# Standing operands of the output and down projections at other byte offsets

## What is computed

```python
gates = jax.nn.sigmoid((h @ w_gate[l]).reshape(B, S, N_BRANCHES, D) + b_gate[l])
mixed = jnp.sum(gates * up, axis=2) @ w_out[l]          # w_out 2048 x 2048
x = x + rmsnorm(mixed, g[1])
h = rmsnorm(x, g[2])
m = jnp.square(jax.nn.relu(h @ w_up[l])) @ w_down[l]    # w_down 8192 x 2048
x = x + rmsnorm(m, g[3])
```

## The kernel before

| operand | role | offset |
|---|---|---|
| `op0h`, `op0l` (x0, x1, x2) | move in mode W, stand in mode T | 64 |
| `op1h`, `op1l` (pool, conv, mix, hidden, att, four) | move in mode W, stand in mode T | 64 |
| `whi`, `wlo` in mode T | move | 64 |
| `whi` in mode W | stands | 128 |
| `wlo` in mode W | stands | 0 |
| the region `big` (`mgh`, `hch`, `vx`, `qt` and others) | both | 64 |

## Time and profile before

### The profile page before, as it was taken

The page is one execution under the profiler, slowest core; times in us unless marked ns, Lnnn a source line. Parts: engine busy times, 40 slices in busy tenths (PEclk is TensorE's granted clock), DMA queues, the critical chain, the costliest instruction groups (busy, mean ns, idle before and its releaser), DMA issues.

```text
span 2187.2 us, 37567 instructions
## 1 busy us (share of the span) xinstructions
PE 2177.7 (100%) x15900; PEld 2046.9 (94%) x15900; DVE 1548.0 (71%) x1895; ACT 1063.0 (49%) x1398; POOL 120.0 (5%) x111
## 2 busy tenths in 40 slices
PE   9999999999999999999999999999999999999998
PEld 9999999999999889989988988998889999999987
DVE  7899588888889577544554555555768787777776
ACT  5444445544444566444543443444555555444443
POOL 1000000000000400000000000000101111110001
PEclk9999999999999999999999999999999999999999
DMA  8876676687787956656656656656755545688784
GB/s 275 245 241 200 201 251 220 228 280 258 256 277 265 244 188 184 193 192 194 196 195 193 194 193 196 200 192 203 246 174 164 164 144 170 224 272 282 256 279 155
DMA packets 248480, 474.97 MB, mean 217 GB/s; under 512 B 21974, under 2 KB 26448, under 8 KB 247544
## 3 DMA queue, kind: packets, MB, share of 16 engines
q1 hardware_dynamic: 243032, 454.40, 65.5%
q0 software_dynamic: 5280, 18.17, 2.9%
HBM read 468.30 MB, written 5.78 MB: 217 GB/s over the span
## 4 chain that ended last, share of the span: by engine, by line
PE 97%; DMA 1%; DVE 1%; ACT 0%; issue 0%; SPq 0%; DVEq 0%; POOLq 0%; POOL 0%; ACTq 0%
PE ps L917 21%; PE ps L918 21%; PE ps L919 21%; PE ps L910 10%; PE ps L911 10%; PE ps L912 10%; PE ps L835 1%; DMA raw<-in_w_out 1%; PE ps L758 0%; PE ps L708 0%; DMA raw<-in_w_in 0%; PE ps L745 0%; PE ps L824 0%; PE ps L823 0%; PE ps L825 0%
## 5 line engine op out<-in xcount | busy, mean ns | idle before, releaser
L917 PE MATMUL ps<-op0h,whiW 128*128 128x256 f32 x3376 | 937.3, 278 | 0.1
L919 PE MATMUL ps<-op0h,wloW 128*128 128x256 f32 x3376 | 932.8, 276 | 0.0
L918 PE MATMUL ps<-op0l,whiW 128*128 128x256 f32 x3376 | 932.7, 276 | 0.0
L1318 DVE TENSOR_TENSOR wloW<-raw,whiW 128x1024 fp32r<-128x1024 f32 (+1 forms) x503 | 618.3, 1241 | 313.5 <-ACT whiW L964 311.1
L964 ACT ACTIVATE whiW<-raw 128x1024 fp32r<-128x1024 f32 (+1 forms) x504 | 529.3, 1058 | 586.0 <-PE ps L919 471.2
L917 PEld LDWEIGHTS ps<-op0h,whiW 128*128 128x128 f32 x3376 | 633.8, 188 | 2.5 <-issue 1.3
L918 PEld LDWEIGHTS ps<-op0l,whiW 128*128 128x128 f32 x3376 | 633.9, 188 | 0.6
L919 PEld LDWEIGHTS ps<-op0h,wloW 128*128 128x128 f32 x3376 | 633.8, 188 | 0.0
L1318 DVE TENSOR_TENSOR wloT<-raw,whiT 128x1024 fp32r<-128x1024 f32 (+1 forms) x264 | 319.1, 1217 | 237.7 <-ACT whiT L964 236.5
L964 ACT ACTIVATE whiT<-raw 128x1024 fp32r<-128x1024 f32 (+1 forms) x264 | 274.0, 1046 | 286.2 <-PE ps L912 228.9
L910 PE MATMUL ps<-whiT,op1h 128*128 128x512 f32 x640 | 249.3, 390 | 0.3 <-DVE wloT L1318 0.3
(11 more groups left out here) (314 smaller groups left out, 2106.8 us busy)
## 6 DMA issues: line engine op xcount, KB each, us to landing
raw<-in_w_in SPq DMA_DIRECT2D x256, 512.0 KB, 4.3
raw<-in_w_up SPq DMA_DIRECT2D x128, 512.0 KB, 3.8
raw<-in_w_down SPq DMA_DIRECT2D x128, 512.0 KB, 4.1
raw<-in_w_ada SPq DMA_DIRECT2D x96, 512.0 KB, 4.6
raw<-in_w_gate SPq DMA_DIRECT2D x96, 512.0 KB, 5.1
raw<-in_w_out SPq DMA_DIRECT2D x64, 512.0 KB, 5.3
raw<-in_w_branch SPq DMA_DIRECT2D x48, 512.0 KB, 5.1
raw<-in_w_proj_a SPq DMA_DIRECT2D x24, 512.0 KB, 5.0
```

Of the source, the lines that this page charges most:

```text
L917: pe.matmul(o, wh, xh[:, ka, :], start=first and m % 2 == 0, stop=False, skip_group_check=True)
L918: pe.matmul(o, wh, xl[:, ka, :], start=False, stop=False, skip_group_check=True)
L919: mm = pe.matmul(o, wl, xh[:, ka, :], start=False, stop=last, skip_group_check=True)
L1318: v.tensor_tensor(wlo[job.mode][q % NSPL][:, :, 0:job.n], x, h.bitcast(F32), ALU.subtract).then_inc(s_lo, 1)
```

## The change

The activations' high and low parts of `mix` and of the four hidden blocks get tensors of their own that overlap `op1h` and `op1l` at shifted addresses. The offsets past a multiple of 256 (256 is the same as 0) are: `mix` 128 and 0 (high and low), `hid0` 128 and 0, `hid1` 0 and 128, `hid2` 64 and 192, `hid3` 192 and 64. 448 bytes are added behind. All instructions, waits and loads stay as they are.

```diff
         op1h, op1l = sb("op1h", [128, 16, 256], F32R), sb("op1l", [128, 16, 256], F32R)
+        def standing(name, high, low):
+
+            return (at(f"{name}h", [128, 16, 256], op1_at - 64 + high, F32R), at(f"{name}l", [128, 16, 256], op1_at + 16576 + low, F32R))
+
+        mixh, mixl = standing("mix", 128, 256)
+        hidden = [standing("hid_a", 128, 256), standing("hid_b", 256, 128), standing("hid_c", 64, 192), standing("hid_d", 192, 64)]
+        top[0] += 448
         tmp_at = top[0]
...
-        hi_of = {..., "mix": op1h, "hid0": op1h, "hid1": op1h, "hid2": op1h,
-                 "hid3": op1h, ...}
+        hi_of = {..., "mix": mixh, "hid0": hidden[0][0], "hid1": hidden[1][0], "hid2": hidden[2][0],
+                 "hid3": hidden[3][0], ...}
...
-                    act.activation(op1h[:, k:k + 2, :], mx[:, k:k + 2, :], ACT.Copy).then_inc(s_mixh, 1)
+                    act.activation(mixh[:, k:k + 2, :], mx[:, k:k + 2, :], ACT.Copy).then_inc(s_mixh, 1)
...
-                    act.activation(op1h[:, k:k + 2, :], half(tmp[2 + u % 4]), ACT.Copy).then_inc(s_hhi, 1)
+                    act.activation(hidden[blk][0][:, k:k + 2, :], half(tmp[2 + u % 4]), ACT.Copy).then_inc(s_hhi, 1)
```

More of the change, by code:

```diff
@@ L403, in program @@
         fgb = at("fgb", [128, 2048], op1_at)
[L404 to L407, removed]
+        hi_of = {"x0": op0h, "x1": op0h, "x2": op0h, "pool": op1h, "conv": op1h, "mix": mixh, "hid0": hidden[0][0], "hid1": hidden[1][0], "hid2": hidden[2][0],
+                 "hid3": hidden[3][0], "att": op1h, "four": op1h, "ya": yah, "ctx": hch, "mg": mgh}
+        lo_of = {"x0": op0l, "x1": op0l, "x2": op0l, "pool": op1l, "conv": op1l, "mix": mixl, "hid0": hidden[0][1], "hid1": hidden[1][1], "hid2": hidden[2][1],
+                 "hid3": hidden[3][1], "att": op1l, "four": op1l, "ya": yal, "ctx": hcl, "mg": mgl}
         columns = {}
@@ L1732, in ep_br @@
                         v.wait_ge(s_mixh, 2 * c + i + 1)
-                        v.tensor_tensor(op1l[:, k:k + 2, :], mx[:, k:k + 2, :], op1h[:, k:k + 2, :].bitcast(F32), ALU.subtract).then_inc(s_mix, 1)
+                        v.tensor_tensor(mixl[:, k:k + 2, :], mx[:, k:k + 2, :], mixh[:, k:k + 2, :].bitcast(F32), ALU.subtract).then_inc(s_mix, 1)
             def ep_wo(job, b0, b1):
@@ L1757, in ep_up @@
                     v.wait_ge(s_hhi, u + 1)
-                    v.tensor_tensor(op1l[:, k:k + 2, :], half(tmp[2 + u % 4]), op1h[:, k:k + 2, :].bitcast(F32), ALU.subtract).then_inc(s_hid, 1)
+                    h, l = hidden[blk]
+                    v.tensor_tensor(l[:, k:k + 2, :], half(tmp[2 + u % 4]), h[:, k:k + 2, :].bitcast(F32), ALU.subtract).then_inc(s_hid, 1)
             def ep_dn(job, b0, b1):
```

## The result

The changed kernel takes 2199.69 us (2199.32 to 2200.58) where the kernel before takes 2188.46 beside it: ratio 1.0051, 95% interval 1.0034 to 1.0069. It is 11 us slower; 9.7 us faster had been forecast. The span of the profiled execution is 2198.1 us.

What follows compares the result with a forecast made beforehand. TensorE's matmul spacing was taken as the bound; 7.68 + 2.56 - 0.56 = 9.7 us gained, giving 2179.3 us against the profiled execution and a median of 2178.9 us (-0.44%), range 2175.0 to 2189.4.

Steps and rivals of the forecast that it cites:

- What bounds the kernel: Whole kernel: matmul spacing on TensorE sets the time, busy 2177.7 of 2187.2 us; neither loads nor VectorE or ScalarE do.
- That the address sets the pitch, by the distance to the moving operand: TensorE matmuls: each standing-tile load takes 16 cycles from the moving stream, 16 more if at the moving operand's offset.
- The strided tile of `ub`: 512-column matmuls at 64 and 64, standing tile spread over twice the bytes: 233.3 ns, 48 cycles over, so loads aren't hidden.
- Distance 64 at -6.67 ns: Output and down projections: 1152 matmuls moved to distance 64 save 6.67 ns each, 7.68 us.
- A distance of 64 either way: `mix`, `hid0`, `hid1`: standing at 128 or 0 counts alike, both 64 from the moving operand.
- 384 matmuls unchanged: `hid2` and `hid3`: 256 and 128 matmuls stay at 64 and were counted as unchanged.
- Distance 128 as for 64: `hid2` and `hid3`: 384 matmuls moved to 192 taken at -6.67 ns each, 2.56 us gained.
- the third rival: 512-column matmuls: whole excess goes for every tile leaving 64, 1536 x 13.3 ns; 2169.1 us, chance 0.05.
- The gap in `wo0`: Output projection: some 84 faster matmuls only reach a late chunk earlier; gap grows some 0.5 us, 0.56 us gain lost.
- Writes and what lies behind at nothing: VectorE and ScalarE writes (at most 4 us uncovered) and moved temporaries (-0.2 to +1.3 us) both costed at zero.
- the fifth: 512-column matmuls: a tile at another offset costs what the spread tile does, +6.7 ns; 2198.8 us, chance 0.08.
- The fourth rival: No change: 512-column matmuls go by 17/16 of the columns, whatever the offset; 2188.6 us, chance 0.15.

Runs made afterwards that it cites:

- the first experiment: Against the kernel before: standing operands back at 64 and 64, the 448 bytes behind kept; 2189.89 us, ratio 1.0005 (0.9995 to 1.0014).

## Why the prediction was wrong

- *What bounds the kernel*: right. TensorE's pitch sets the time (it is busy for 2188.2 of 2198.1 us in the changed kernel), and little hid the loss (0.7 us at the gap in `wo0`).
- *That the address sets the pitch, by the distance to the moving operand*: right in the main, though the 17/16 of the columns (544 cycles for 512, 272 for 256) spoke for no change. The strided tile of `ub`, 233.3 ns against 226.7, was a hint that loads are not hidden.
- *Distance 64 at -6.67 ns*: this step failed. It took mode W's 16 cycles over at 256 columns for 512 columns. At distance 0 the excess is 32 at 256, 384 and 512 columns (29 at 272), and the prediction took the load's part of the excess to be the same at every width for all loads. At distance +64 it is 16, 32 and 48 at 256, 384 and 512 columns. Measured, in place of -6.67: +5.2 ns in `dn0`, +6.6 in `dn1`. Nor do mode W's 16 cycles belong to distance 64 as such: there 128 and 128, and 0 and 0, take 117.8 ns, 27 over.
- *"A distance of 64 either way"*: wrong. At 512 columns a tile 64 past the moving operand costs 6.6 ns more, one 64 short of it 2.2.
- *384 matmuls unchanged*: wrong. They stay at 64 but not at their pitch. If they had, the 128 moved loads of `dn2` would carry its 1.7 us alone, 13 ns each, where 192 and 192 costs 5.7.
- *Distance 128 as for 64*: the two are close (232.4 against 233.3 ns), but dear, not cheap.
- *The rows*: the 119 ns of `o23` comes from 12 matmuls; over all 48 of that part it is 119.9, 32 cycles over. The 215.6 ns of plain float32 is not a whole matmul: line 835 issues two matmuls on `vx` and two on `vc` for a head, and the trace has four rows and four. A plain float32 matmul of 256 columns takes two rows, 431 ns, some four cycles a column and not two. A row still spans 512 cycles with 5 over, but it is not a matmul that streams 512 columns, so it is weak support for the third rival.
- *The gap in `wo0`*: it was to grow with faster matmuls. They came slower, and it vanished; its 0.7 us are the only gain of the change.
- *Writes and what lies behind at nothing*: right, within what was measured. VectorE and ScalarE are as busy as before (1547.8 and 1063.8 us), and what lies behind costs at most 3 us by the interval of the first experiment, with all its down stages at their old pitch.
- *The rivals*: the fifth, priced by the strided tile at +6.7 ns, gave 2198.8 us, 0.9 from the result. It had 8 chances in 100, because the cheaper rows of mode W were held against it, and those were rows of another width. That it came so near in size is in part luck: it put one price on each moved tile and none on the rest, the measured prices run from 2.2 to 6.6 ns and fall on the unmoved ones too, and no run ties the strided tile's price to that of an offset. The fourth rival's rule, 17/16 of the columns, holds only as the lowest that was seen: no stage of float32r matmuls in any run went under it (272 cycles for 256 columns, 544 for 512), and the forecast's 220.0 ns lay under it.

What stays open is why the excess at distance 0 is constant while that at distance +64 grows with the columns, why two parts at different offsets cost more than each by itself, and what keeps one of two pitches at one pair of addresses. The runs show all three; none shows the mechanism.

## What to carry to other kernels

A price read at one width of the moving operand isn't one for another width (64 bytes of offset cost +6.6 ns at 512 columns, nothing at 384 and -6.7 ns at 256): look for a row that has both the placement and the width, and where none exists, let the range reach as far up as down. Where TensorE runs without waits, place standing and moving operand by measurement for each width: here the same offset for both at 512 columns of float32r (226.7 ns, against 228.9 to 234.3 for the other offsets); at 256 columns the same offset is the dearest (120.0 ns), but a different one gave 113.3 ns in some stages and 117.8 to 119.1 in others. When several placements are to be compared, give each a whole stage and read the stage's time over its count of matmuls.

## What was not expected of the hardware

- The offset of the standing against the moving operand, past a multiple of 256 bytes, changes the pitch of float32r matmuls by up to 3% at 512 columns (226.7 to 233.3 ns, to 234.3 at an offset of 160) and 6% at 256 (113.3 to 120.0). The sign counts: +6.6 ns at +64, +2.2 at -64.
- High and low part at different offsets cost more than the prices of both say: 64 and 128 takes 231.1 ns, not 228.9.
- The order of the offsets turns over between these widths, with 173.3 ns at distance 0 and +64 for 384 columns.
- At 256 columns in mode W the same addresses ran at 113.3 and, after eight transposes, at 118.9 ns.
- Loading half a tile (64 of 128 columns) made a 512-column matmul slower at distance 0, 230.0 against 226.7 ns, and hardly faster at +64, 232.6 against 233.3.
